# Filter network's angles in turns, and the hyena chain's steps one projection job later, in a hybrid mixer + MoE layer

## What is computed

```python
def hyena_filters(seq, w1, b1, w2, b2, w3, b3, freq, w4):
    z = jnp.concatenate([t, jnp.cos(ang), -jnp.sin(ang)], axis=-1)
    hdn = jnp.sin(freq * (z @ w1 + b1))
    hdn = jnp.sin(freq * (hdn @ w2 + b2))
    hdn = jnp.sin(freq * (hdn @ w3 + b3))
    h = (hdn @ w4).reshape(seq, HY_ORDER, 2, HY_WIDTH)
    return h * window[:, None, None, :]

def hyena_mixer(u, conv_w, conv_b, filters, d_bias):
    u = dwconv(u, conv_w, conv_b)              # 3 taps, per channel
    v, x1, x2 = jnp.split(u, 3, axis=-1)
    z = v
    for n, xg in enumerate((x1, x2)):
        z = xg * (bidir_long_conv(z, filters[:, n, 0], filters[:, n, 1]) + d_bias[n] * z)
    return z

def conformer_conv(u, dw_w, dw_b, ln_g, ln_b):
    a, g = jnp.split(u, 2, axis=-1)
    u = dwconv(a * jax.nn.sigmoid(g), dw_w, dw_b)     # 31 taps, per channel
    return jax.nn.silu(layernorm(u, ln_g, ln_b))
```

## Time and profile before

| | before |
|---|---|
| median of 3 runs | 1289.26 us (1288.73 to 1289.8) |
| the profiled execution, its own time | 1291.79 us |
| its span, first to last instruction | 1290.0 us |
| mean granted TensorE clock | 0.995 |
| PE busy | 1213.5 us, 94% |
| DVE busy | 410.2 us, 32% |
| ACT busy | 174.0 us, 13% |
| POOL busy | 33.1 us, 3% |
| HBM read | 474.22 MB |

### The profile page before, as it was taken

One profiled execution on the slowest core, in us unless ns is written; L12 is line 12 of the kernel. 1 busy time (PEld: TensorE's weight loads), 2 busy tenths in 40 slices (PEclk: granted clock), 3 DMA queues, 4 the chain that ended last, 5 costly groups with the idle time before them and its releaser, 6 DMA issues.

```text
span 1290.0 us, 13991 instructions
## 1 busy us (share of the span) xinstructions
PE 1213.5 (94%) x5550; PEld 577.2 (45%) x5550; DVE 410.2 (32%) x774; ACT 174.0 (13%) x311; POOL 33.1 (3%) x50
## 2 busy tenths in 40 slices
PE   6999999999999999999999998999899999989897
PEld 1777478888544343333333332433333333334332
DVE  5178896884422221120222102111301211021203
ACT  3222004230221010010101001000101010010000
POOL 3300200001000000000000000000000000000000
PEclk9999999999999999999999999999999999999999
DMA  9943442779489999999999999999999999999996
GB/s 373 383 174 108 148 156 107 301 286 401 179 354 426 401 428 428 428 429 428 428 430 429 427 428 429 428 428 430 429 428 428 429 428 428 430 429 427 427 426 247
DMA packets 50707, 475.73 MB, mean 369 GB/s; under 512 B 3970, under 2 KB 4130, under 8 KB 24051
## 3 DMA queue, kind: packets, MB, share of 16 engines
q1 hardware_dynamic: 49426, 471.26, 87.8%
q0 software_dynamic: 1248, 4.03, 0.9%
HBM read 474.22 MB, written 1.05 MB: 368 GB/s over the span
## 4 chain that ended last, share of the span: by engine, by line
PE 66%; DMA 28%; DVE 2%; ACT 1%; issue 1%; SPq 0%; DVEq 0%
DMA ring_sb<-w_down 26%; PE bank L1149 20%; PE bank L1249 11%; PE bank L859 10%; PE bank L1104 5%; PE bank L1265 4%; PE bank L1020 3%; PE bank L868 3%; PE bank L1049 2%; DMA area_sb<-w_down 2%; PE bank L1118 1%; DVE area_sb L1867 1%; PE bank L784 1%; PE bank L798 1%; PE bank L1010 1%
## 5 line engine op out<-in xcount | busy, mean ns | idle before, releaser
L1149 PE MATMUL bank<-ring_sb,area_sb 128*64 128x512 f32 x1536 | 400.2, 598 | 16.4 <-DMA ring_sb<-w_gu 16.4
L1149 PEld LDWEIGHTS bank<-ring_sb,area_sb 128*64 128x64 f32 x1536 | 124.4, 137 | 226.1 <-issue 213.7
L1249 PE MATMUL bank<-ring_sb,area_sb 128*64 128x512 f32 x608 | 165.9, 598 | 18.7 <-DMA ring_sb<-w_down 16.8
L1149 PE MATMUL bank<-area_sb 128*64 128x512 f32 x512 | 171.2, 594 | 0.0
L859 PE MATMUL bank<-area_3h_sb,ring_sb 128*128 128x256 f32 x704 | 154.2, 379 | 0.0
L859 PEld LDWEIGHTS bank<-area_3h_sb,ring_sb 128*128 128x128 f32 x704 | 133.2, 190 | 20.1 <-issue 1.8
L2123 DVE TENSOR_SCALAR area_sb<-bank 128x512 f32<-128x512 f32 x32 | 22.1, 692 | 304.2 <-PE bank L1149 304.2
L2147 DVE TENSOR_TENSOR area_sb<-area_sb,bank 128x512 f32<-128x512 f32 x64 | 44.0, 688 | 211.9 <-PE bank L1265 211.9
L2154 DVE TENSOR_TENSOR area_sb<-bank,area_sb 128x512 f32<-128x512 f32 x32 | 22.1, 692 | 230.4 <-PE bank L1249 218.0
L1249 PEld LDWEIGHTS bank<-ring_sb,area_sb 128*64 128x64 f32 x608 | 51.2, 137 | 89.7 <-issue 89.7
L1509 ACT ACTIVATE area_sb<-bank 128x512 f32<-128x512 f32 (+1 forms) x80 | 44.0, 551 | 333.5 <-PE bank L1104 255.6
(11 more groups left out here) (278 smaller groups left out, 807.8 us busy)
## 6 DMA issues: line engine op xcount, KB each, us to landing
ring_sb<-w_gu SPq DMA_DIRECT2D x96, 2048.0 KB, 26.2
ring_sb<-w_down SPq DMA_DIRECT2D x38, 2048.0 KB, 25.8
area_sb<-w_gu SPq DMA_DIRECT2D x32, 2048.0 KB, 30.3
area_sb<-w_down SPq DMA_DIRECT2D x16, 2048.0 KB, 20.4
ring_sb<-w_in SPq DMA_DIRECT2D x14, 2048.0 KB, 10.1
ring_sb<-w_ada SPq DMA_DIRECT2D x12, 2048.0 KB, 10.3
area_3h_sb<-w_down SPq DMA_DIRECT2D x8, 2048.0 KB, 35.6
ring_sb<-w_branch SPq DMA_DIRECT2D x3, 2048.0 KB, 9.5
```

The costliest lines, as they stand in the source:

```text
L1149: ins = pe.matmul(bank[n][r, :], xT[:, k, r], w[e][:, n * 512:(n + 1) * 512], start=False, stop=k == KT - 1, skip_group_check=True)
L1249: ins = pe.matmul(bank[4 + n][r, :], hidT[:, k, e * SLOTS:(e + 1) * SLOTS], w[e][:, kk, n * 512:(n + 1) * 512], start=False, stop=k == KT ...
```

## The change

In the filter network the angle is kept in turns: `freq` is divided by 2 pi once (a new column `freq_turns`), the nearest whole number is found by adding and subtracting a large constant, and the difference goes to the sine with a negative scale. Six operations behind the first become two. In the rest, jobs, PE's order, ACT's order and DVE's order are changed: hy3 goes ahead of the first transform, hy4 and hy5 ahead of the first return, q0 ahead of the second transform, q1 and k0 ahead of the second return, k1 ahead of the transposes; short_conv and the taps of `conv` are placed anew. q0 and k0 keep their place in the order in which DVE empties banks.

```diff
-PI_A, PI_B, PI_C = 6.28125, 0.0019350051879882812, 3.0199159819e-07
 ROUND = 12582912.0
@@ front_jobs
-    jobs += [("hyT00", "act"), ("hyT01", "act")]
+    jobs += [("hyT00", "act"), ("hyT01", "act"), ("hy3", "act")]
     jobs += [("u00", "act"), ("u01", "dve"), ("u02", "act"), ("u03", "dve")]
-    jobs += [("hy3", "act"), ("hy4", "act"), ("inv00", "dve"), ("inv01", "dve"), ("hyT10", "act"), ("hyT11", "act")]
-    jobs += [("hy5", "act"), ("u10", "act"), ("u11", "dve"), ("u12", "act"), ("u13", "dve")]
-    jobs += [("hyT20", "act"), ("hyT21", "act"), ("q0", "dve"), ("q1", "dve"), ("inv10", "dve"), ("inv11", "dve")]
-    jobs += [("k0", "dve"), ("zT0", "act"), ("zT1", "act"), ("k1", "dve"), ("v0", "dve"), ("v1", "dve")]
+    jobs += [("hy4", "act"), ("hy5", "act"), ("inv00", "dve"), ("inv01", "dve"), ("hyT10", "act"), ("hyT11", "act")]
+    jobs += [("q0", "dve"), ("u10", "act"), ("u11", "dve"), ("u12", "act"), ("u13", "dve")]
+    jobs += [("hyT20", "act"), ("hyT21", "act"), ("q1", "dve"), ("k0", "dve"), ("inv10", "dve"), ("inv11", "dve")]
+    jobs += [("k1", "dve"), ("zT0", "act"), ("zT1", "act"), ("v0", "dve"), ("v1", "dve")]
@@ order of emptying
+for _name, _next in (("q0", "q1"), ("k0", "k1")):
+    EVICTIONS.remove(_name)
+    EVICTIONS.insert(EVICTIONS.index(_next), _name)
@@ PE
             turn_hyena(0)
+            hyena_in(3)
             wait_emptied(pe, "hyT01")
             to_frequency(0)
-            for i in (3, 4):
+            for i in (4, 5):
                 hyena_in(i)
             to_time(0)
             turn_hyena(1)
-            hyena_in(5)
+            token_major("q0", 0, 0)
             wait_emptied(pe, "inv01")
             to_frequency(1)
             turn_hyena(2)
-            for t in range(TT):
-                token_major(f"q{t}", 0, t)
+            token_major("q1", 0, 1)
+            token_major("k0", 1, 0)
             to_time(1)
-            token_major("k0", 1, 0)
+            token_major("k1", 1, 1)
...
-            token_major("k1", 1, 1)
@@ ACT
-                act.activation(mlp_y[:, 3, :], mlp_y[:, 0, :], ACT.Sin).then_inc(sin_done, 1)
+                act.activation(mlp_y[:, 3, :], mlp_y[:, 0, :], ACT.Sin, scale=-2.0 * 3.1415925).then_inc(sin_done, 1)
...
             hyena_turned(0)
+            hyena_out(3)
             even_part(0)
-            hyena_out(3)
             hyena_out(4)
+            hyena_out(5)
             hyena_turned(1)
-            hyena_out(5)
@@ DVE
+            step(dve.tensor_scalar(freq_turns, hf_col[:, 3:4], 1.0 / (2 * math.pi), None, ALU.mult))
+            step.wait()
             for n in range(3):
                 b = product(dve, f"mlp{n}")
-                emptied_here(dve.tensor_scalar(y, b[:, 0:SEQ], hf_col[:, n:n + 1], hf_col[:, 3:4],
+                emptied_here(dve.tensor_scalar(y, b[:, 0:SEQ], hf_col[:, n:n + 1], freq_turns,
                                                ALU.add, ALU.mult))
                 emptied_here.wait()
-                step(dve.tensor_scalar(turns, y, 1.0 / (2 * math.pi), ROUND, ALU.mult, ALU.add))
-                step.wait()
-                step(dve.tensor_scalar(turns, turns, -ROUND, None, ALU.add))
-                for part_of_pi in (PI_A, PI_B, PI_C):
-                    step.wait()
-                    step(dve.scalar_tensor_tensor(y, turns, -part_of_pi, y, ALU.mult, ALU.add))
-                step.wait()
-                dve.tensor_scalar(y, y, 3.1415925, -3.1415925, ALU.min, ALU.max).then_inc(sin_asked, 1)
+                step(dve.tensor_scalar(turns, y, ROUND, None, ALU.add))
+                step.wait()
+                dve.scalar_tensor_tensor(y, turns, -ROUND, y, ALU.add, ALU.subtract).then_inc(sin_asked, 1)
...
             conv(8, 12)
+            short_conv(2)
+            conv(12, 16)
             mix(0)
-            short_conv(2)
             short_conv(3)
-            conv(12, 13)
+            short_conv(4)
+            conv(16, 18)
             hyena_step(0)
-            short_conv(4)
-            conv(13, 15)
             short_conv(5)
+            conv(18, 21)
             mix(1)
             dve.wait_ge(attn_landed, 16 * 4)
             add_bias(0)
+            conv(21, 22)
             hyena_step(1)
-            conv(15, 24)
+            conv(22, 24)
             add_bias(1)
             conv(24, TAPS)
```

More of the change, by code:

```diff
@@ L350, in build_layer @@
         c_col = small[:, 180:181]
+        freq_turns = small[:, 181:182]
         top_s = small[:, 188:194].rearrange("p (t k) -> p t k", t=TT)
```

## The result

| | before | after |
|---|---|---|
| median | 1289.85 us (1288.73 to 1294.29, 7 runs) | 1296.09 us (1294.46 to 1298.31, 7 runs) |
| ratio | 1 | 1.0042 [1.0031 to 1.0052] |
| the profiled execution, its own time | 1291.79 us | 1294.46 us |
| its span | 1290.0 us | 1292.3 us |
| mean granted TensorE clock | 0.995 | 0.991 |

The change makes the kernel slower, by 0.42%. The forecast was slower by 0.2%, 1291.9 us, with a range up to 1294.5. The two profiled executions differ by 2.67 us, as summed (+2.6); the medians differ by 6.2, and the ratio makes 5.4. So the account of the mechanism holds, and the account of what it is measured against does not. (Most lines are three higher: L859 is now L862, L868 L871, L893 L896, L1104 L1107.)

A forecast was written before the change was run, and what follows sets the result against it. The weight stream bounds the kernel from about 540 us, PE before, so front shifts pass to the end one for one. +0.7 + 2.3 - 0.4 = +2.6 us gives 1291.9 us from the 1289.26 median; 8-in-10 range 1288.0 to 1294.5.

The forecast's parts named there:

- The wait at k0: PE waits 5.4 us at k0 until add_bias behind mix 1 empties q0's bank; 4.7 us ahead becomes +0.7.
- The Trainium skill's rule on rotating banks: Speaks against the edit: between q0 and k0 the new order puts nothing but work that DVE delays.
- The first rival: q0's bank is emptied before PE reaches k0 at 137.9; PE keeps 4.7 us: -5.1, 1284.2 us; chance 0.14.
- The clock behind that wait: At k0's products, the clock falls after the 5.4 us wait: +2.3 us, taken between 1.96 and 2.9.
- The second rival: The wait at k0 is there but the clock stays full or recovers at once: +0.3, 1289.6 us; chance 0.10.
- What is late next: After k0, centring stays ahead of PE's variance with 1.2 us slack; the shift passes unchanged to gate 8 and the end.
- The filter network: At the start, sine 1 comes 3.4 us sooner but loads bound what follows: -0.4 us, between -1.0 and +0.1.
- the 2.1 us wait and the clock's fall go: Ahead of and in the first transform, hy3 covers ACT's copies: 2.1 us wait and 1.96 us of slow clock vanish.

The follow-up runs named there:

- e2: The changed kernel with k0 and inv10 exchanging banks, nothing else: 1288.08 us, 0.9975 of before.
- e9: The kernel before with the 2.1 us wait ahead of the first transform stretched to 5.8 us by six repeated ACT copies: 1297.35 us, 1.0047 of before.
- e4: The kernel before with the new filter network alone: 1291.83 us, 1.0007 of before.
- e6: The kernel before with two extra products filling PE's 2.1 us wait ahead of the first transform: 1291.60 us, 0.9999 of before.
- e3: The changed kernel with six extra products keeping PE busy in the wait ahead of k0: 1295.50 us, 1.0032 of before.
- e7: The changed kernel with the old filter network, so the new order alone: 1295.18 us, 1.0031 of before.
- e5: The kernel before, unchanged, run again for a second trace: 1292.93 us (1 run).

## Why the forecast was right in kind and too small

Step by step, as the prediction put them:

- **The wait at k0** ("job 8 ahead", q0's bank behind mix 1): right. 5.4 us summed, 5.48 measured, released by the DVE line named; e2 removes it with one line. PE's and DVE's schedules hold within 0.5 us: mix 0 at 101.2 (101.6), mix 1 at 129.5 (129.9), k0 at 143.0 (143.3), an idle DVE of 1.3 us ahead of mix 1.
- **The Trainium skill's rule on rotating banks** (Perfetto Trace Analysis, Optimizing Tensor Performance, Matmuls), by which emptying one bank should lie under the products of the next group: the traces agree. With the banks in turn but emptying late, 1.0037; with k0 on a bank emptied in time, 0.9975. The first rival, 5.1 us under before, is what e2 shows in kind; by the ratio it is worth 3.2, since 1.7 of its 4.7 us were the clock's fall.
- **The clock behind that wait**, "+2.3": 1.6 to 2.9 in four traces, mean 2.3, and 2.9 in e9. That the mean is hit so closely is in part luck. The value was taken between a row of 1.96, of which 0.26 is not the clock's, and the start of the kernel, where the profile has the granted clock at 1.00 from 5 to 26 us, so that no row shows the slow products there to be the clock's doing. k0's extra 0.26 us, which come with any clock, stand nowhere in the sum. The second rival, no fall, happened in none of the five long waits.
- **What is late next**: nothing, as forecast. The centring and the variance kept their slack, since gate 8 came 2.62 us late and no more, and the shift reached the gather: 323.16 - 320.25 = 2.9.
- **The filter network**, "-0.4": sine 1 comes 3.6 us sooner, ada 1 waits for its load at 17.98 and then takes 3.26 us. The spectrum starts at 28.20 (28.52 before), and in other traces with the new network at 27.42 to 29.63. The projections start at 41.7 on average with either network (six traces with the new, seven with the old). The term is nothing, not -0.4.

**The step that failed** is a term of the sum: "the 2.1 us wait and the clock's fall go", 1.96 us counted as a gain of the change. The wait is gone in every trace of the new order; the fall was in one of the three traces of the kernel before, and not in e4's. The sum compared the changed kernel with an execution that had lost 1.7 us by chance. Against that one it comes out (front +2.9 measured, 0.7 + 2.3 summed). Against the front that three other traces and e6 show, 318.5, the four traces of the changed chain give 323.5 on average: +5.0. Then the sum was moved to the runs' median, as if the fall were in that as well. With the fall counted at nothing, the sum is 2.6 + 1.7 = 4.3 (3.9, if it comes in one execution of four); with k0's 0.3 us behind the wait and no gain from the filter network (+0.4) it is 5.0, where the ratios 1.0037 and 1.0042 make 4.8 and 5.4 us. The unlucky trace had its own time near the median all the same, because its last body ran at a full clock, which others don't (below): its total hid that its front was long. A second trace, or the length of each part, would have shown it.

Two smaller things stay beside the sum. The time outside the span is 1.7 to 1.9 us in every execution with the old filter network and 1.9 to 2.3 in those with the new one (up to 3.0 in e3), so some 0.2 to 0.4 us of the loss are there; no run shows why. And the median given before the change, 1289.26 of three runs, lies 2 us below that of the 57 later ones, which moved the forecast's number but not its ratio.

## What to carry to other kernels

When jobs are moved in a list whose buffers go round, look up for each moved job which one had its buffer before, and where the emptying engine stands with that: a rotation is of use only if no long step of that engine lies in between, and exchanging two buffers can turn a loss of 0.4% into a gain of 0.25%. A fall of the clock in a single trace may be an event of that execution: before it is counted as a gain, look for it in a second trace, and compare part by part, since two chance events can cancel in the total.

## What the runs showed of the hardware

**The same short wait lowers the clock in some executions only.** 2.1 us before the first transform: 5.40 us in one trace, 3.70 in three. Waits of 5.5 and 5.8 us lowered it in five of five. Between 42 us and the first gather the clock leaves 1.00 in these six places and nowhere else in the 13 traces. In the first trace of the kernel before it was still at 1.00 in the wait, and fell when the products behind it had begun (the earlier trace rows has 0.57 for 93 to 97):

```profile
91.00:93.00 2.00, 0.20 (x2) 0.01 (x1) 2.00 (x6) 1.97 (x5) 0.00 (x0) 1.00 0.00 0
```

**What a long wait costs depends on how far the low stretch reaches into the work behind it**, 1.6 to 2.9 us here. In the first trace of the changed kernel the clock fell in the wait, before k0 began:

```profile
140.00:142.00 2.00, 0.00 (x0) 0.00 (x0) 1.97 (x4) 0.00 (x0) 0.00 (x0) 0.55 1.02 411
```

Between 146 and 149 us its mean is 0.83, which makes the low level last until 147.0. That is 4.0 us behind k0's start at 143.03, of which half is lost: 2.0 us, as k0's length shows. In e7 k0 starts at 142.83, and the mean of the same stretch is 0.55:

```profile
146.00:149.00 3.00, 3.00 (x5) 1.18 (x4) 0.00 (x0) 0.00 (x0) 0.00 (x0) 0.55 0.00 0
```

So the level is low until 148.7, 5.9 us behind the start, and half of it is 2.9. The Trainium skill (TensorE: Matmul & The Clock Gate, Part 1) says that the number of slow products at a kernel's start varies from run to run; behind these waits in mid-kernel the traces show the same.

**The same happens late in the loop.** The first group of the last body's down projection starts behind a wait of 1.9 us for its weights, in each of the three traces below. In the chain of waits of the kernel before, first trace:

```profile
1266.14 3.65 PE bank L1249 x16
```

of e5:

```profile
1264.34 6.61 PE bank L1249 x16
```

and of e2:

```profile
1262.35 5.35 PE bank L1255 x16
```

Three microseconds lie between 3.65 and 6.61 for the same 16 products, and it is the clock again. Busy time by stretch of the kernel before, first trace:

```profile
1266.00:1268.00 2.00, 1.85 (x10) 0.86 (x12) 1.73 (x6) 0.00 (x0) 0.00 (x0) 1.00 1.03 410
```

and of e5:

```profile
1264.00:1267.00 3.00, 2.66 (x8) 0.92 (x10) 1.94 (x6) 0.00 (x0) 0.00 (x0) 0.50 1.03 412
```

From the first gather to the end of the span the kernel before takes 927.8, 930.9 and 930.6 us in its three traces, the changed one 927.5, 927.2 and 929.5. So a part of the spread of one kernel's executions is there. Whether the changed chain favours one of the cases, which would explain why some ratios show less than the fronts (4.0 us for 5.6 in e7), these few traces don't tell.
